# A column unit between FoX's turned probabilities and its values, and FoX's second tile and MoBA's turns at other places among the recurrence's column units

## The chip, the cores and the metric

The kernel runs on one core of one Trainium2 chip. The metric is the device time of one execution in microseconds. Before the change it is 1789.96 us, the median of three runs (1787.77 to 1790.02).

## The reference, cut to what matters

Two different transformer blocks, each with two layers, over a sequence of 256 tokens of width 1024, all in fp32. The edits lie in the mixer stage of the first block, which runs once in each of its two layers. There one projection of the normed input, `z = rms_norm(x, mix_norm[l]) @ mix_w_in[l]`, feeds three mixers side by side:

```python
z_fox, z_moba, z_rwkv = jnp.split(z, [FOX_IN, FOX_IN + MOBA_IN], axis=-1)
y_fox  = fox_mixer(z_fox, ...)    # 4 heads of 64: softmax(q k^T / 8 + c_i - c_j, causal) v
y_rwkv = rwkv7_mixer(z_rwkv, ...) # 8 heads of 64: a recurrence over tokens with decay and a rank-one correction
y_moba = moba_mixer(z_moba, ...)  # 4 heads of 64, rotary on 16 dims: at 256 tokens one causal block
y = jnp.concatenate([y_fox, y_rwkv, y_moba], axis=-1) @ mix_w_out[l]
```

For each of FoX and MoBA: scores of a tile of 128 queries, mask, softmax, product with the values. For the recurrence: r, k and v of width 512, each blended with the token before (`zf + (z_prev - zf) * mu`), then decays, normed keys, and the recurrence itself, which the kernel does in chunks of 64 tokens with small matmuls. Behind the mixers stand a projection with a residual, a cross attention and a feed-forward layer.

## The kernel before, in words

**Weights.** All large weights come as one stream of 546 units of up to 256 x 512 fp32 (512 KB). SP loads them into a ring of four places (`raw`). For each unit ScalarE copies it, rounded, to `whi` (`act_split`, L339) and VectorE writes the rest, `raw - whi`, to `wlo` (`dve_split`, L380). Each product is then three matmuls: high by high, high by low, low by high (L400 to L402; in a column unit L421 to L423). ScalarE's copy of unit u waits until TensorE has used unit u - 4; SP's load waits for VectorE's split of it.

**Tokens.** 256 tokens are two tiles of 128 (`t` or `qt` is 0 or 1).

**Column units.** The recurrence's k, r and v are projected turned, with channels on partitions: `pe_rw_cols(l, n, banks)` does unit n (0 to 3) of one of them, 24 matmuls of 128 x 256, into two PSUM banks. k and v use banks 0 and 1, r banks 4 and 5. After the four units of one, VectorE scales the two banks (`dve_rw_scale`, L993), ScalarE multiplies by 1 - mu (`act_rw_mix`, L1000) and VectorE adds the token before times mu (`dve_rw_mix`, L1009).

**FoX and MoBA.** A tile goes through these steps (`fox` True or False):

- TensorE turns queries and keys (`pe_at_turn`, L809, for FoX; `pe_mo_turn`, L1646, for MoBA, both into bank 6 for each tile, so the second waits until ScalarE has copied the first); ScalarE copies them out (L815).
- `pe_at_scores`: TensorE, L1707, and for FoX the forget term in L1711.
- `dve_at_scores`: VectorE scales and masks (L1725, and for the second tile L1728), row maximum (L822), its negative, the "shift" (L824).
- `act_at_exp`: ScalarE, four exponentials with row sums (L830).
- `pe_at_probs`: TensorE turns the probabilities (L844) in groups of four; ScalarE copies the even groups (`act_at_probs`, L851), VectorE the odd (`dve_at_probs`, L858, after the reciprocal of the sums, L863).
- `pe_at_values`: TensorE (L872), `dve_at_values`: VectorE multiplies by the reciprocals (L880).

**Keys of the recurrence.** `pe_rw_length` (L1083) sums squares, `dve_rw_keys_k` is one product of 128 x 1024 (L1117), `dve_rw_keys` makes the normed keys (L1126, four instructions, whose last MoBA's first turn waits for) and two products (L1132, L1136). After the column units come `pe_rw_products` (L1214) with masks on VectorE (L1227), then five levels of a triangular inverse (L1266, L1278, with L1285 on ScalarE and L1293 on VectorE), a bonus and gate part (L1424, L1436, L1437) and the chunks (L1312 and on).

**Order.** Every engine has its own list, written by hand, and runs it strictly in order: `pe_mix` (L2130), `act_mix` (L2238), `dve_mix` (L2340), `pool_mix`. The engines meet only by semaphores. No planner moves anything; an operation that waits holds all that stands behind it in its engine's list.

Of the kernel before, what the change touches and what calls it, by code (L numbers as in the profile page):

```python
# [131 lines left out]
class Program:  # L132
# [1997 lines left out]
    def pe_mix(self, l):  # L2130
        pe = self.nc.tensor
        for n in range(4):
            self.pe_rw_low(l, n)
            if n < 2:
                self.pe_turn_x(("mix", l), self.TURN_BANKS["mix"], self.x_done(l, "ffn1", 1), 4 + 2 * n, 2)
        self.pe_mix_spread(l)
        queries, keys, values = (self.pe_z(l, g) for g in (1, 2, 3))
        next(queries)
        self.pe_rw_low_turn(l)
        next(queries)  # L2140
        next(queries)
        self.pe_rw_lora(l)
        next(queries)
        self.pe_rw_cum(l, 0)
        self.pe_rw_cum(l, 1)
        for n in range(4):
            next(keys)
        for n in range(4):
            next(values)
        for sem, value in self.z_done(l, 2):  # L2150
            pe.wait_ge(sem, value)
        self.pe_rw_cols(l, 0, (0, 1))
        self.pe_rw_cols(l, 1, (0, 1))
        self.pe_at_turn(l, 0)
        self.pe_rw_cols(l, 2, (0, 1))
        self.pe_at_logs(l)
        self.pe_at_turn(l, 1)
        self.pe_rw_cols(l, 3, (0, 1))
        self.pe_at_scores(l, True, 0)
        pe.wait_ge(*self.rw_act("exp -cum", l, 0))  # L2160
        self.pe_rw_cols(l, 0, (4, 5))
        self.pe_rw_cols(l, 1, (4, 5))
        self.pe_rw_length(l)
        self.pe_at_probs(l, True, 0)
        self.pe_at_values(l, True, 0)
        self.pe_at_scores(l, True, 1)
        self.pe_rw_cols(l, 2, (4, 5))
        self.pe_rw_cols(l, 3, (4, 5))
        self.pe_mo_turn(l, 0)
        self.pe_at_probs(l, True, 1)  # L2170
        pe.wait_ge(*self.rw_dve("square sum", l, 1))
        self.pe_rw_cols(l, 0, (0, 1))
        self.pe_at_values(l, True, 1)
        self.pe_mo_turn(l, 1)
        self.pe_rw_cols(l, 1, (0, 1))
        self.pe_at_scores(l, False, 0)
        self.pe_rw_cols(l, 2, (0, 1))
        self.pe_rw_cols(l, 3, (0, 1))
        self.pe_at_probs(l, False, 0)
        self.pe_rw_products(l, 0, (0, 1))  # L2180
        self.pe_at_values(l, False, 0)
        self.pe_rw_products(l, 0, (2, 3))
        self.pe_at_scores(l, False, 1)
        self.pe_kv(l, 0, 0)
        self.pe_rw_products(l, 1, (0, 1, 2, 3))
        self.pe_kv(l, 0, 1)
        self.pe_at_probs(l, False, 1)
        self.pe_rw_by_token(l, "v", self.VT, (5, 7), [self.rw_dve("mixed", "v", l, 3), self.rw_dve("masked", l, 1, 1),
                                                      self.rw_dve("masked", l, 1, 3)])
        self.pe_at_values(l, False, 1)  # L2190
        self.pe_kv(l, 0, 2)
        self.pe_rw_level(l, 1)
        self.pe_rw_level(l, 2)
        self.pe_rw_by_token(l, "b", self.E3, (5, 7), [self.rw_act("by token", "v", l, 1), self.rw_dve("b end", l)])
        self.pe_rw_level(l, 3)
        self.pe_rw_by_token(l, "k", self.E2, (5, 7), [self.rw_act("by token", "b", l, 1), self.rw_dve("k end", l)])
        self.pe_rw_level(l, 4)
        self.pe_rw_bonus(l, 3)
        self.pe_rw_gate(l, 0, 2)
        self.pe_rw_level(l, 5)  # L2200
        pe.wait_ge(*self.rw_act("bonus", l))
        self.pe_rw_gate(l, 1, 3)
        self.pe_rw_first(l)
        self.pe_rw_early(l, 0, 0)
        self.pe_rw_u(l, 0, 0)
        self.pe_kv(l, 0, 3)
        self.pe_rw_state(l, 0, 0)
        self.pe_kv(l, 1, 0)
        self.pe_rw_rhs(l, 0, 1)
        self.pe_rw_early(l, 0, 1)  # L2210
        self.pe_rw_u(l, 0, 1)
        self.pe_kv(l, 1, 1)
        self.pe_rw_state(l, 0, 1)
        self.pe_kv(l, 1, 2)
        self.pe_rw_rhs(l, 1, 0)
        self.pe_rw_early(l, 1, 0)
        self.pe_rw_u(l, 1, 0)
        self.pe_kv(l, 1, 3)
        self.pe_rw_state(l, 1, 0)
        self.pe_kv_keys(l, 0)  # L2220
        self.pe_kv_keys(l, 1)
        self.pe_rw_rhs(l, 1, 1)
        self.pe_wo_a_turn(l, 0)
        self.pe_rw_u(l, 1, 1)
        self.pe_wo_a_turn(l, 2)
        self.pe_rw_state(l, 1, 1)
        self.pe_wo_a(l, 0, 0)
        self.pe_wo_a(l, 0, 1)
        self.pe_wo_a(l, 1, 0)
        self.pe_turn(("wo_b", l), [[self.Y[:, t, k * P:(k + 1) * P] for t in range(NT)] for k in range(4)], (4, 5, 6, 7),  # L2230
                     [self.rw_dve("out", l, 1)], kt0=4)
        self.pe_wo_a(l, 1, 1)
        self.pe_gemm((0, 1), 4, kt0=4, key=("wo_b", l), first=False)
        self.pe_gemm((2, 3), 4, kt0=4, key=("wo_b", l), first=False, units=(0,))
        self.pe_early("xa", l, self.x_done(l, "mix", 0))
        self.pe_gemm((2, 3), 4, kt0=4, key=("wo_b", l), first=False, units=(1,))

    def act_mix(self, l):  # L2238
# [45 lines left out]
        self.act_split(1)  # L2284
        self.act_mo_turn(l, 0)
        self.act_at_probs(l, True, 1)
        self.act_rw_mix(l, "r", self.RT, PV_OMR)
        self.act_split(2)
        self.act_mo_turn(l, 1)
        self.act_split(1)  # L2290
        self.act_at_exp(l, False, 0)
        self.act_split(1)
# [47 lines left out]
    def dve_mix(self, l):  # L2340
# [39 lines left out]
        self.dve_at_probs(l, True, 0)  # L2380
        self.dve_rw_length(l)
        self.dve_split(1)
        self.dve_at_values(l, True, 0)
        self.dve_rw_keys_k(l)
        self.dve_at_scores(l, True, 1)
        self.dve_rw_keys(l)
        self.dve_split(1)
# [1217 lines left out]
```

## Time and profile before

| | |
|---|---|
| median of three runs | 1789.96 us (1787.77 to 1790.02) |
| profiled execution | 1789.94 us, span 1788.6 us |
| TensorE, matmul | 1765.4 us busy, 99% of the span |
| TensorE, weight load | 1476.6 us, 83% |
| VectorE | 1155.0 us, 65% |
| ScalarE | 945.4 us, 53% |
| GpSimd | 128.3 us, 7% |
| mean granted TensorE clock | 0.998 |
| DMA | 301.12 MB, mean 168 GB/s |

Times are from the start of the span. Matmuls overlap in the pipe, so each one's duration is longer than its step to the next, and a busy TensorE is not one at its peak. The step from one start to the next is what counts in the timeline. In brackets behind an operation stands the idle time of its engine just before it and what ended it. The stretch with the edits is from about 262 to 300 us in layer 0 and lies 620 us later in layer 1.

### The profile page before, as it was taken

What the parts mean: (1) busy time and instruction counts of PE and PEld (TensorE: products, weight loads), DVE (VectorE), ACT (ScalarE), POOL (GpSimd) and SP (SyncE); (2) the same over time, 40 slices, a digit from 0 to 9 for tenths busy, and PEclk for the clock granted to TensorE, in tenths of its full rate; (3) what the DMA queues carried; (4) which work ended last, traced back from release to release, by engine and by line L of the source; (5) the groups of instructions that cost most, each with busy time, mean ns of one, the idle gap of its engine ahead of it and who ended that gap; (6) DMA issues with size and microseconds to landing.
All of it is one profiled execution on the core that took longest, in us unless ns stands there. A gap on an engine that the chain in (4) does not pass through costs nothing.

```text
span 1788.6 us, 26360 instructions
## 1 busy us (share of the span) xinstructions
PE 1765.4 (99%) x10762; PEld 1476.6 (83%) x10762; DVE 1155.0 (65%) x1589; ACT 945.4 (53%) x1433; POOL 128.3 (7%) x90
## 2 busy tenths in 40 slices
PE   9999999999999999999999999999999999999999
PEld 6888888888888888888888878888888888888887
DVE  5555678676555565556786755555697557697556
ACT  6454675345544454447653554444646554656553
POOL 0100010141000000000002210000002000002000
PEclk9999999999999999999999999999999999999999
DMA  8755542134555557555421436555554455554564
GB/s 285 279 190 186 173 152 85 61 105 130 187 185 186 186 187 253 186 169 188 142 84 61 140 116 223 189 188 170 165 180 156 166 193 193 174 177 153 174 190 130
DMA packets 84343, 301.12 MB, mean 168 GB/s; under 512 B 9728, under 2 KB 10880, under 8 KB 83712
## 3 DMA queue, kind: packets, MB, share of 16 engines
q1 hardware_dynamic: 80192, 289.44, 49.1%
q10 hardware_dynamic: 3712, 8.56, 1.4%
q8 instruction: 85, 1.39, 0.3%
q0 software_dynamic: 320, 1.45, 0.3%
q14 instruction: 34, 0.28, 0.0%
HBM read 298.36 MB, written 1.05 MB: 167 GB/s over the span
## 4 chain that ended last, share of the span: by engine, by line
PE 88%; DVE 6%; ACT 4%; issue 1%; DMA 1%; POOL 0%; SPq 0%; DVEq 0%; ACTq 0%
PE ps L400 25%; PE ps L402 25%; PE ps L401 25%; DVE wlo L380 1%; ACT whi L339 1%; PE ps L623 1%; PE ps L1278 1%; PE ps L1266 1%; DMA raw<-stream 1%; DVE a_lo L476 1%; PE ps L2680 1%; PE ps L809 1%; PE ps L460 1%; PE ps L423 1%; PE ps L421 1%
## 5 line engine op out<-in xcount | busy, mean ns | idle before, releaser
L380 DVE TENSOR_TENSOR wlo<-raw,whi 128x1024 fp32r<-128x1024 f32 (+1 forms) x545 | 668.9, 1236 | 360.1 <-ACT whi L339 358.6
L339 ACT ACTIVATE whi<-raw 128x1024 fp32r<-128x1024 f32 (+1 forms) x545 | 570.7, 1053 | 454.2 <-PE ps L402 423.7
L400 PE MATMUL ps<-whi,a_hi 128*128 128x512 f32 x1712 | 677.2, 396 | 5.9 <-DVE a_lo L2013 2.0
L402 PE MATMUL ps<-whi,a_lo 128*128 128x512 f32 x1712 | 664.7, 388 | 0.0
L401 PE MATMUL ps<-wlo,a_hi 128*128 128x512 f32 x1712 | 663.7, 388 | 0.0
L400 PEld LDWEIGHTS ps<-whi,a_hi 128*128 128x128 f32 x1712 | 321.5, 188 | 74.5 <-issue 4.7
L402 PEld LDWEIGHTS ps<-whi,a_lo 128*128 128x128 f32 x1712 | 321.3, 188 | 67.6
L401 PEld LDWEIGHTS ps<-wlo,a_hi 128*128 128x128 f32 x1712 | 321.9, 188 | 61.6
L400 PE MATMUL ps<-whi,h_hi 128*128 128x512 f32 x336 | 131.6, 392 | 0.0
L402 PE MATMUL ps<-whi,h_lo 128*128 128x512 f32 x336 | 130.9, 390 | 0.0
L401 PE MATMUL ps<-wlo,h_hi 128*128 128x512 f32 x336 | 130.8, 389 | 0.0
L400 PEld LDWEIGHTS ps<-whi,h_hi 128*128 128x128 f32 x336 | 63.1, 188 | 13.6 <-issue 0.7
L402 PEld LDWEIGHTS ps<-whi,h_lo 128*128 128x128 f32 x336 | 63.1, 188 | 13.2
L421 PE MATMUL ps<-a_hi,whi 128*128 128x256 f32 x256 | 73.9, 289 | 0.0
L401 PEld LDWEIGHTS ps<-wlo,h_hi 128*128 128x128 f32 x336 | 63.1, 188 | 12.9
L423 PE MATMUL ps<-a_hi,wlo 128*128 128x256 f32 x256 | 72.4, 283 | 0.0
L422 PE MATMUL ps<-a_lo,whi 128*128 128x256 f32 x256 | 72.3, 283 | 0.0
L645 ACT ACTIVATE arena<-ps,small 128x256 f32<-128x256 f32 x88 | 36.9, 471 | 65.6 <-PE ps L402 65.5
L553 POOL TENSOR_TENSOR small<-small,minus_half 128x2 f32<-128x2 f32 x9 | 6.3, 701 | 858.1 <-DVE small L546 642.3
L691 DVE SCALAR_TENSOR_TENSOR arena<-ps,small,arena 128x256 f32<-128x256 f32 x88 | 38.5, 480 | 38.4 <-ACT arena L645 38.4
L652 ACT ACTIVATE h_hi<-ps 128x256 fp32r<-128x256 f32 x72 | 23.7, 382 | 57.4 <-PE ps L623 57.4
L790 POOL TENSOR_TENSOR small<-small,minus_half 128x16 f32<-128x16 f32 (+1 forms) x14 | 39.2, 2803 | 166.3 <-DVE small L2622 80.5
(330 smaller groups left out, 1680.6 us busy)
## 6 DMA issues: line engine op xcount, KB each, us to landing
raw<-stream SPq DMA_DIRECT2D x545, 512.0 KB, 3.4
arena<-rows ACTq DMA_DIRECT2D x2, 1026.0 KB, 13.8
arena<-mem_turned ACTq DMA_DIRECT2D x2, 1024.0 KB, 9.1
arena<-lora ACTq DMA_DIRECT2D x2, 768.0 KB, 6.6
arena<-x_turned SPq DMA_DIRECT2D x4, 256.0 KB, 6.4
x_res<-x SPq DMA_DIRECT2D x2, 512.0 KB, 9.4
arena<-mem ACTq DMA_DIRECT2D x1, 1024.0 KB, 12.2
arena<-rows ACTq DMA_DIRECT2D x2, 512.0 KB, 4.6
```

The costliest lines, as they stand in the source:

```text
L339: self.split_hi.mark(act.activation(self.weights(self.whi, u), self.weights(self.raw, u), ACT.Copy), u)
L380: self.split_lo.mark(dve.tensor_tensor(self.weights(self.wlo, u), self.weights(self.raw, u), self.weights(self.whi, u).bitcast(F32), ALU.s ...
L400: pe.matmul(out, a_h, hi, start=start, stop=False, skip_group_check=True)
L401: pe.matmul(out, a_h, lo, start=False, stop=False, skip_group_check=True)
L402: last = pe.matmul(out, a_l, hi, start=False, stop=True, skip_group_check=True)
L421: pe.matmul(out, hi, self.AHI[:, kt, :], start=first and kt == 0, stop=False, skip_group_check=True)
L422: pe.matmul(out, hi, self.ALO[:, kt, :], start=False, stop=False, skip_group_check=True)
L423: last = pe.matmul(out, lo, self.AHI[:, kt, :], start=False, stop=True, skip_group_check=True)
L645: self.silu.mark(act.activation(self.SG[:, t, :], self.bank((2 if j == 1 else 4) + t, 256), ACT.Silu, scale=self.rs(0, t)), key, j, t)
L652: self.ht_hi.mark(act.activation(self.h_place(j)[0][:, kk, :], self.bank(self.h_bank(j, kk), S), ACT.Copy), key, j, kk)
L691: self.h_ready.mark(dve.scalar_tensor_tensor(self.h_buffer(j)[:, t, :], self.bank((2 if j == 1 else 4) + t)[:, 256:512], self.rs(0, t), se ...
L790: m.mark(pool.tensor_tensor(x, x, self.minus_half[:, 0:x.shape[1]], ALU.pow), key)
```

## The change

Only the order of calls in the three lists. On TensorE unit 2 of r is moved from behind FoX's second scores to between FoX's first turned probabilities and first values; unit 0 of v, with its wait, from behind FoX's second turned probabilities to before MoBA's first turn; and FoX's second values from before MoBA's second turn to behind unit 1 of v. On ScalarE the copy of MoBA's second turn goes from behind the blends of r and two splits to before them. On VectorE the product L1117 goes before FoX's first values.

```diff
@@ pe_mix
         self.pe_at_probs(l, True, 0)
+        self.pe_rw_cols(l, 2, (4, 5))
         self.pe_at_values(l, True, 0)
         self.pe_at_scores(l, True, 1)
-        self.pe_rw_cols(l, 2, (4, 5))
         self.pe_rw_cols(l, 3, (4, 5))
+        pe.wait_ge(*self.rw_dve("square sum", l, 1))
+        self.pe_rw_cols(l, 0, (0, 1))
         self.pe_mo_turn(l, 0)
         self.pe_at_probs(l, True, 1)
-        pe.wait_ge(*self.rw_dve("square sum", l, 1))
-        self.pe_rw_cols(l, 0, (0, 1))
-        self.pe_at_values(l, True, 1)
         self.pe_mo_turn(l, 1)
         self.pe_rw_cols(l, 1, (0, 1))
+        self.pe_at_values(l, True, 1)
         self.pe_at_scores(l, False, 0)
@@ act_mix
         self.act_at_probs(l, True, 1)
+        self.act_mo_turn(l, 1)
         self.act_rw_mix(l, "r", self.RT, PV_OMR)
         self.act_split(2)
-        self.act_mo_turn(l, 1)
@@ dve_mix
         self.dve_split(1)
+        self.dve_rw_keys_k(l)
         self.dve_at_values(l, True, 0)
-        self.dve_rw_keys_k(l)
         self.dve_at_scores(l, True, 1)
```

## Rows read from the trace of the kernel before

**Rows 1.** The page, busy us by engine (share of the span) x instructions.

```profile
PE 1765.4 (99%) x10762; PEld 1476.6 (83%) x10762; DVE 1155.0 (65%) x1589; ACT 945.4 (53%) x1433; POOL 128.3 (7%) x90
```

**Rows 2.** Chain of waits, 262 to 345 us: start us, us, what.

```profile
269.13 1.09 PE ps L1711 x8
...
270.31 0.42 DVE arena L1725
...
295.74 0.34 DVE arena L880
...
296.21 1.13 PE ps L1707 x8
```

**Rows 3.** Timeline of TensorE, layer 0: start us, us, operation [idle before, releaser].

```profile
265.61 0.60 PE L844 MATMUL ps<-const_tables,arena 128*128 128x128 f32 x4
266.99 1.08 PE L872 MATMUL ps<-arena 128*128 128x64 f32 x8 [0.78 <-ACT arena L851]
...
270.12 0.39 PE L421 MATMUL ps<-a_hi,whi 128*128 128x256 f32 x1
...
275.98 0.60 PE L1646 MATMUL ps<-const_tables,arena 128*128 128x128 f32 x4
276.41 1.04 PE L844 MATMUL ps<-const_tables,arena 128*128 128x128 f32 x8
...
280.15 1.89 PE L872 MATMUL ps<-arena 128*128 128x64 f32 x16
281.88 0.61 PE L1646 MATMUL ps<-const_tables,arena 128*128 128x128 f32 x4
...
285.70 0.71 PE L1707 MATMUL ps<-arena 64*128 64x128 f32 x8 [0.34 <-ACT arena L815]
...
292.21 0.60 PE L844 MATMUL ps<-const_tables,arena 128*128 128x128 f32 x4
...
296.21 1.13 PE L1707 MATMUL ps<-arena 64*128 64x256 f32 x8 [0.30 <-DVE arena L880]
```

**Rows 4.** Timeline of VectorE, layer 0.

```profile
270.31 0.42 DVE L1725 SCALAR_TENSOR_TENSOR arena<-ps,const_tables 128x256 f32<-128x256 f32 x1 [0.58 <-PE ps L1711]
...
273.10 1.67 DVE L1126 SCALAR_TENSOR_TENSOR arena<-arena 128x256 f32<-128x256 f32 x4
...
277.38 1.22 DVE L380 TENSOR_TENSOR wlo<-raw,whi 128x1024 fp32r<-128x1024 f32 x1
...
284.10 0.42 DVE L880 TENSOR_TENSOR arena<-ps,small 128x256 f32<-128x256 f32 x1
284.43 1.22 DVE L380 TENSOR_TENSOR wlo<-raw,whi 128x1024 fp32r<-128x1024 f32 x1
...
289.34 0.17 DVE L824 TENSOR_SCALAR small<-small 128x4 f32<-128x4 f32 x1
...
295.65 0.41 DVE L880 TENSOR_TENSOR arena<-ps,small 128x256 f32<-128x256 f32 x1
```

**Rows 5.** Timeline of ScalarE, layer 0.

```profile
276.61 0.60 ACT L815 ACTIVATE arena<-ps 128x512 f32<-128x512 f32 x1 [0.36 <-PE ps L1646]
```

**Rows 6.** Timeline of VectorE, layer 1.

```profile
890.45 0.42 DVE L1725 SCALAR_TENSOR_TENSOR arena<-ps,const_tables 128x256 f32<-128x256 f32 x1 [0.58 <-PE ps L1711]
```

**Rows 7.** Stretches: length, busy by engine, PEclk, DMA; then the chain of waits.

```profile
336.00:340.00 4.00, 4.00 (x82) 4.00 (x80) 0.26 (x1) 1.19 (x2) 0.00 (x0) 0.51 0.01 4
...
956.00:960.00 4.00, 4.00 (x72) 2.42 (x70) 2.56 (x3) 0.61 (x2) 0.00 (x0) 1.00 0.02 4
...
331.79 0.96 PE ps L1436 x2
...
342.89 1.01 PE ps L1312 x29
...
951.95 0.96 PE ps L1436 x2
...
959.95 1.01 PE ps L1312 x29
```

## The prediction

> **What bounds the kernel now.** I read the page's busy times first: TensorE's matmuls are busy for 1765.4 us, 99% of the span [rows 1]. That share says little about one stage, since a modelled end of a matmul covers short waits. So I read next the chain of waits through the mixers of layer 0, where all edits lie. It does not stay on TensorE. It leaves TensorE with the last matmul of FoX's scores for the second tile (L1711, ends 270.22), goes to VectorE (L1725, 270.31) and stays there, but for a few pieces of ScalarE that VectorE's own results released, until the normalised values of MoBA's first tile (L880, 295.74). There it returns to TensorE, with the scores of MoBA's second tile at 296.21 [rows 2]. So for 26 us the end is set by VectorE's queue, and its start by the moment at which TensorE delivers those FoX scores. The timelines say the same from both sides. VectorE sat idle for 0.58 us before L1725, on TensorE's L1711 [rows 4]. TensorE has three small holes: 0.78 us before FoX's first values (ScalarE's copy of the turned probabilities), 0.34 us before MoBA's first scores (ScalarE's L815, the copy of MoBA's turned tile 1), 0.30 us before MoBA's second scores (VectorE's L880) [rows 3]. Layer 1 has the same 0.58 us at 890.45 [rows 6]; one layer is worked out and doubled.
>
> **The change part by part.** No instruction, wait or DMA is added or dropped; the order on three queues changes. The weight units keep their order, so the split work and SP's queue of loads see the same sequence; POOL's queue is untouched.
>
> Edit 1, TensorE: column unit 2 of r goes between FoX's turned probabilities and values of tile 0. A unit takes 2.93 us: two of them fill 270.12 to 275.98 [rows 3]. Eight transposes and one unit take 276.41 to 280.15, 3.74 us, so a transpose takes 0.10 us [rows 3]. After the change the four transposes run from 265.61 to 266.0, the unit until 268.94. Its weights are ready: the unit's split stands ahead of the first FoX scores in VectorE's order. ScalarE's copy had ended by 266.99, where the values started before; they now start at 268.94 without a wait. The hole of 0.78 us is filled, which with the idle start of the pipe is 0.98 us of the unit's 2.93 us; the other 1.95 us stand in front. The values and the scores of tile 1 take the 3.13 us from 266.99 to 270.12 [rows 3]. So these scores end at 272.07 instead of 270.12.
>
> That is the step that costs. Before, the unit stood behind the scores and ran while VectorE scaled and reduced them. VectorE now starts L1725 at 270.31 + 1.95 = 272.26. Has it something to do meanwhile? Edit 2 moves its product k w (L1117) ahead of FoX's values; both ran before the scores anyhow, so nothing more is brought into the hole. I cost edit 2 at nothing: what hides it is the wait for the scores itself. Without that cover (had the values been late on the chain) it could cost or save up to its own 1.2 us; it is not late.
>
> Behind L1725 everything on VectorE is in order and moves with it: L1126 from 273.10 to 275.05, the split of the second v unit from 277.38 to 279.33, FoX's second values from 284.10 to 286.05, the split of the fourth v unit from 284.43 to 286.38, MoBA's shift from 289.34 to 291.29, MoBA's first values from 295.65 to 297.60 [rows 4]. The two waits for ScalarE that lie in between (blends of r, the split after MoBA's exponentials) follow pieces of this same chain and move too.
>
> Edit 3, TensorE, the rest: r's unit 3 runs 272.07 to 275.0, v's unit 0 to 277.93; then MoBA's turn 0, which needs L1126's four products (276.72 by the shift), 0.43 us to 278.36 [rows 3, 4]; FoX's eight transposes to 279.17. Turn 1 waits for ScalarE's copy of turn 0. Before, that copy began 0.63 us after the turn did and took 0.60 us [rows 3, 5]: 1.23 us against 0.43 + 0.81 = 1.24 us of turn and transposes, so the wait is between 0 and 0.2 us. Turn 1 ends near 279.6. Then v's unit 1 needs its split, which VectorE ends at 279.33 + 1.22 = 280.55: a new wait of 0.95 us. The unit ends at 283.5, the values of tile 1 (1.73 us, 280.15 to 281.88) at 285.2; VectorE wants them at 286.05, 0.8 us later. MoBA's first scores follow at once: turn 1 was copied long before, so the hole of 0.34 us goes. From 285.70 to 292.21 they and two units took 6.51 us [rows 3], now ending at 291.7; the fourth unit's split is ready at 287.6, a microsecond ahead of its use. Next come MoBA's transposes, which need exponentials that move by 1.95 us: TensorE waits, at most 1.95 + 0.5 = 2.4 us. MoBA's second scores then wait for L880 and start at 296.21 + 1.95 = 298.16.
>
> Edit 4, ScalarE: the copy of turn 1 goes ahead of the blends of r. Costed at nothing: ScalarE has nothing to do there until VectorE scales r, which is itself 1.95 us later. If TensorE were later than that, ScalarE would hold the blends, up to the 0.60 us of the copy.
>
> From 298.16 on TensorE runs without another of these waits, and all that VectorE and ScalarE bring it is shifted by the same amount, so nothing gives it back. Sum: 2 x 1.95 = 3.9 us. Bounds for a layer: nothing, if VectorE absorbs it; 2.93 us, if the filled hole brings nothing. I take 1.95 us, since both ends of the chain are read from rows. The profiled execution took 1789.94 us around its span and the median of the runs is 1789.96 us, so the base needs no correction: 1789.94 + 3.9 = **1793.8 us**.
>
> **The rivals.** *R1, TensorE's own stream decides.* If VectorE's queue had more air than its records show, only TensorE's holes count. The change fills 0.78 and 0.34 us, and with 0.30 us if VectorE is in time, 1.42 us a layer, 2.8 us in all: 1787.1 us. For it: TensorE's 99%. Against: the chain leaves TensorE exactly at the scores, and the 0.30 us show VectorE behind TensorE at the end of the stretch. It decides once the scores' delay stays under VectorE's slack; the row of 0.58 us shows that slack to be below zero.
>
> *R2, absorbed.* The later scores are made good inside the stretch, by about what the filled holes give, or the two effects cancel: 1790 us. For it: six queue places change at once and half a microsecond here and there is not in my sum. Against: no queue gets shorter.
>
> *R3, the clock.* In layer 0 the granted clock was 0.51 from 336 to 340 us, TensorE's lower level of 1.2 GHz, and 1.00, its 2.4 GHz, at the same place of layer 1 [rows 7]. The same work took 342.89 - 331.79 = 11.10 us in layer 0 and 959.95 - 951.95 = 8.00 us in layer 1 [rows 7]. Ahead of both stood the same run of 64x64 matmuls, so it is a matter of when this work comes, and the change moves it by 1.95 and 3.9 us. One fall is worth 3.1 us: none makes 1793.8 - 3.1 = 1790.7 us, two make 1796.9 us. For it: two layers alike in all but this; and the runs shown reach from 1787.77 to 1790.02, a step of 2.2 us. Against a lasting effect: it would be drawn anew in each run, and the median would keep to the commoner number. The Trainium skill (TensorE: Matmul & The Clock Gate, "What's actually happening") says that the gate follows how busy the array has been, and looks at it on a schedule that runs freely and does not start with the kernel. By that rule identical work may fall or not, as the trace's two layers do, and the time is 3.1 us lower or higher by the draw alone, as R3.
>
> **How the numbers follow.** This kernel's measurement can tell 0.2%, 3.6 us, from no change; my 3.9 us lie just above it. Chances: forecast with one fall as before 0.52; R3 with none 0.15, with two 0.10; R2 0.13; R1 0.10. Of the forecast's 0.52, 0.42 come out slower by more than 3.6 us and 0.10 within. Slower: 0.42 + 0.10 (two falls) = 0.52. Within: 0.10 + 0.15 + 0.13 + 0.03 (part of R1) = 0.41. Faster: 0.07, R1 with a fall less. The range leaves out R1 and what lies beyond two falls: 1789.5 to 1797.0 us. The forecast's own range is 1792.5 to 1795.5.
>
> **What would show it.** In the changed profile, in each layer: no wait before L872 at about 269, where the 0.78 us stood; L1711 ends 1.9 to 2.0 us later against L844 at 265.6, and the idle time of VectorE before L1725 is about 2 us, in two parts (before L880, and before L1725); a new wait of some 1 us before the first L421 behind the second turn, on VectorE's split; no wait on L815 before MoBA's scores; a wait of 1 us or more on ScalarE's L830 before MoBA's transposes; the one on L880 grows from 0.30 us to about 1 us; the first L1266 comes 1.95 us later in layer 0 and 3.9 us later in layer 1. I am wrong if the first L1266 comes at its old place or earlier (R1, R2), or if it comes as said and the end doesn't (R3).

## The result and the profile after

The changed kernel takes 1791.74 us, the median of 19 runs (1789.75 to 1793.65), against 1787.77 us for the kernel before (1786.22 to 1791.12, 19 runs). The ratio is 1.0019 with a 95% interval of 1.0013 to 1.0025: slower by 3.4 us, 2.3 to 4.5. The change is clear of no change, but lies at the prediction's line of 0.2%, 3.6 us, and not clearly on either side of it. The profiled execution took 1791.55 us, with a span of 1790.2 us.

The best measure here is a stretch within one profile, from the first L1083 (sums of squares) to the first L1266 (the triangular inverse). All edits lie in it, and the granted clock was 1.00 throughout it in both kernels.

| start, us | first L1083 | first L1266 | stretch |
|---|---|---|---|
| before, layer 0 | 263.88 | 311.41 | 47.53 |
| before, layer 1 | 884.02 | 931.57 | 47.55 |
| changed, layer 0 | 263.46 | 312.82 | 49.36 |
| changed, layer 1 | 882.33 | 931.69 | 49.36 |

The four rows of layer 0, TensorE's timeline, the kernel before first:

```profile
263.88 1.89 PE L1083 MATMUL ps<-arena,const_tables 128*128 128x256 f32 x8
311.41 2.08 PE L1266 MATMUL ps<-arena 64*64 64x64 f32 x64
...
263.46 1.89 PE L1083 MATMUL ps<-arena,const_tables 128*128 128x256 f32 x8
312.82 2.08 PE L1266 MATMUL ps<-arena 64*64 64x64 f32 x64
```

So the change costs 1.83 us in layer 0 and 1.81 us in layer 1, 3.6 us in all. None of it is given back behind the stretch: from the first L1083 of layer 0 to that of layer 1 the changed kernel takes 882.33 - 263.46 = 618.87 us, and turn_early, one of the experiments below, 880.65 - 263.68 = 616.97 us. Its stretch is within 0.03 us as long as that of the kernel before, and its granted clock was 1.00 from one L1083 to the other, as that of the changed kernel was.

The timeline of TensorE in the changed kernel, layer 0; the columns are start, length, operation, and in brackets the idle time before it and what ended it.

```profile
265.19 0.60 PE L844 MATMUL ps<-const_tables,arena 128*128 128x128 f32 x4
265.55 0.36 PE L421 MATMUL ps<-a_hi,whi 128*128 128x256 f32 x1
...
268.50 1.00 PE L872 MATMUL ps<-arena 128*128 128x64 f32 x8
...
271.56 0.39 PE L421 MATMUL ps<-a_hi,whi 128*128 128x256 f32 x1
...
277.41 0.60 PE L1646 MATMUL ps<-const_tables,arena 128*128 128x128 f32 x4
277.84 1.04 PE L844 MATMUL ps<-const_tables,arena 128*128 128x128 f32 x8
278.71 0.64 PE L1646 MATMUL ps<-const_tables,arena 128*128 128x128 f32 x4
...
280.08 0.39 PE L421 MATMUL ps<-a_hi,whi 128*128 128x256 f32 x1 [0.73 <-DVE wlo L380]
...
283.05 1.89 PE L872 MATMUL ps<-arena 128*128 128x64 f32 x16
284.87 0.72 PE L1707 MATMUL ps<-arena 64*128 64x128 f32 x8
...
292.67 0.66 PE L844 MATMUL ps<-const_tables,arena 128*128 128x128 f32 x4 [1.14 <-ACT arena L830]
...
297.63 1.13 PE L1707 MATMUL ps<-arena 64*128 64x256 f32 x8 [1.20 <-DVE arena L880]
```

The two holes of [rows 3] that the change aimed at are gone: no wait before L872, none on L815 before MoBA's scores. Three waits stand there now: 0.73 us for the split of v's unit 1, 1.14 us for the exponentials, and 1.20 us instead of 0.30 for MoBA's first values. From the turned probabilities to the end of FoX's second scores it is 271.56 - 265.19 = 6.37 us instead of 270.12 - 265.61 = 4.51 us [rows 3], 1.86 us more. The same stretch on VectorE:

```profile
267.73 1.22 DVE L1117 TENSOR_TENSOR arena<-arena 128x1024 f32<-128x1024 f32 x1
269.61 0.42 DVE L880 TENSOR_TENSOR arena<-ps,small 128x256 f32<-128x256 f32 x1 [0.67 <-PE ps L872]
271.75 0.42 DVE L1725 SCALAR_TENSOR_TENSOR arena<-ps,const_tables 128x256 f32<-128x256 f32 x1 [1.71 <-PE ps L1711]
...
274.53 1.67 DVE L1126 SCALAR_TENSOR_TENSOR arena<-arena 128x256 f32<-128x256 f32 x4
...
285.52 0.42 DVE L880 TENSOR_TENSOR arena<-ps,small 128x256 f32<-128x256 f32 x1
...
297.07 0.41 DVE L880 TENSOR_TENSOR arena<-ps,small 128x256 f32<-128x256 f32 x1
```

VectorE idles 0.67 + 1.71 us where it idled 0.58 us [rows 4]: 1.80 us more, which is the loss but for a few hundredths. Behind it the queue is as before, shifted: from L1725 to MoBA's first L880 it is 297.07 - 271.75 = 25.32 us, before 295.65 - 270.31 = 25.34 us [rows 4]. The chain of waits (start, us, what) hands over at the same operations as in [rows 2]:

```profile
270.57 1.09 PE ps L1711 x8
...
271.75 0.42 DVE arena L1725
...
297.15 0.34 DVE arena L880
...
297.63 1.13 PE ps L1707 x8
...
312.89 2.01 PE ps L1266 x64
```

### The profile page after: what moved, and what is told of

Same layout as the page of the kernel before. It is cut to its first block, busy times and chain, and to the rows that moved or that the text cites. A ratio compares the mean times of both kernels' runs of the same rounds, so it can differ in the third digit from the quotient of the medians.

```text
span 1790.2 us, 26360 instructions
## 1 busy us (share of the span) xinstructions
PE 1764.3 (99%) x10762; PEld 1475.6 (82%) x10762; DVE 1156.0 (65%) x1589; ACT 945.2 (53%) x1433; POOL 128.2 (7%) x90
## 4 chain that ended last, share of the span: by engine, by line
PE 89%; DVE 6%; ACT 3%; issue 1%; DMA 1%; POOL 0%; SPq 0%; DVEq 0%; ACTq 0%
PE ps L400 25%; PE ps L402 25%; PE ps L401 25%; DVE wlo L380 1%; PE ps L623 1%; PE ps L1278 1%; DMA raw<-stream 1%; PE ps L1266 1%; PE ps L421 1%; ACT whi L339 1%; PE ps L422 1%; PE ps L423 1%; DVE a_lo L476 1%; PE ps L2680 1%; PE ps L809 1%
## 5 line engine op out<-in xcount | busy, mean ns | idle before, releaser
L421 PEld LDWEIGHTS ps<-a_hi,whi 128*128 128x128 f32 x256 | 48.9, 191 | 3.2 <-DVE wlo L380 1.9
```

What stands on the lines that cost most here:

```text
L421: pe.matmul(out, hi, self.AHI[:, kt, :], start=first and kt == 0, stop=False, skip_group_check=True)
```

## The experiments

Each changes the order of calls in the lists, and nothing else. The stretch is given for layers 0 and 1. Ratios are to the kernel before on the same chip, with their 95% intervals.

| kernel | stretch, us | ratio (interval) |
|---|---|---|
| kernel before | 47.53, 47.55 | |
| whole change | 49.36, 49.36 | 1.0019 (1.0013 to 1.0025) |
| unit_only | 49.40, 49.39 | 1.0019 (1.0010 to 1.0028) |
| unit_back | 49.36, 49.35 | 1.0024 (1.0015 to 1.0032) |
| two_units | 53.11, 52.51 | 1.0053 (1.0040 to 1.0066) |
| product_early | 47.53, 47.52 | 1.0002 (0.9993 to 1.0010) |
| v0_only | 49.36, 49.34 | 1.0017 (1.0008 to 1.0026) |
| values_late | 48.94, 48.95 | 1.0011 (1.0002 to 1.0020) |
| turn_early | 47.50, 47.55 | 1.0001 (0.9992 to 1.0010) |
| key_product_late | 48.10, 48.06 | 1.0004 (0.9995 to 1.0013) |
| scores_first_both | 47.52, 47.56 | 1.0006 (0.9997 to 1.0015) |
| scores_first_turn | 48.29, 46.97 | 1.0003 (0.9994 to 1.0012) |

**unit_only: edit 1 alone.**

```diff
         self.pe_at_probs(l, True, 0)
+        self.pe_rw_cols(l, 2, (4, 5))
         self.pe_at_values(l, True, 0)
         self.pe_at_scores(l, True, 1)
-        self.pe_rw_cols(l, 2, (4, 5))
```

> The kernel before with edit 1 alone: r's unit 2 between FoX's first turned probabilities and first values. Theory: the stretch from the first L1083 to the first L1266 is 49.3 to 49.4 us in both layers, as with the whole change, time 3.6 us over before where the clock is alike (ratio about 1.002). Rival A (the later moves carry the cost): 47.5 us, ratio 1.000. Rival B (the unit costs more and the later moves give some back): over 49.7 us, ratio 1.0025 or more.

As the theory had it: 49.40 and 49.39 us. Without edit 2 VectorE waits 1.80 us before L880 and 0.58 us before L1725, the same sum as in the whole change, so edit 2 is worth nothing. VectorE's timeline:

```profile
269.90 0.42 DVE L880 TENSOR_TENSOR arena<-ps,small 128x256 f32<-128x256 f32 x1 [1.80 <-PE ps L872]
272.04 0.42 DVE L1725 SCALAR_TENSOR_TENSOR arena<-ps,const_tables 128x256 f32<-128x256 f32 x1 [0.58 <-PE ps L1711]
```

**unit_back: the whole change without edit 1.**

```diff
         self.pe_at_probs(l, True, 0)
-        self.pe_rw_cols(l, 2, (4, 5))
         self.pe_at_values(l, True, 0)
         self.pe_at_scores(l, True, 1)
+        self.pe_rw_cols(l, 2, (4, 5))
         self.pe_rw_cols(l, 3, (4, 5))
```

> The changed kernel with r's unit 2 back behind FoX's second scores; every other move stays. Measure: the stretch from the first L1083 to the first L1266, 47.53 us before and 49.36 us changed in layer 0. Theory (the unit ahead of the scores delays VectorE's chain, the other moves cost nothing): 47.4 to 47.6 us, VectorE idle 0.6 us before L1725, the wait of 0.78 us before L872 back, and a time like that of the kernel before (ratio 0.999 to 1.001). Rival A (the later moves, with their new waits on the split of v's unit 1, the exponentials and L880, carry the cost): still 49.0 us or more, ratio 1.001 to 1.002. Rival B (the later moves gain what the unit takes away from them): 46.9 to 47.2 us, ratio 0.999 or less.

The theory's first half fails here: the stretch stays at 49.36 us, as rival A had it, though unit_only shows edit 1 to cost the whole sum too. The number is rival A's, but the wait is not one of the three that it named. VectorE's timeline shows a wait at a place where before there was none:

```profile
269.71 0.42 DVE L1725 SCALAR_TENSOR_TENSOR arena<-ps,const_tables 128x256 f32<-128x256 f32 x1 [0.61 <-PE ps L1711]
...
279.76 0.69 DVE L858 COPY arena<-ps 128x512 f32<-128x512 f32 x1 [1.69 <-PE ps L844]
```

The scores come in time, but now three column units stand on TensorE between them and FoX's turned probabilities, and L858, next in VectorE's queue, waits 1.69 us for these.

**v0_only and values_late: which of the later moves it is.** They split edit 3. The first moves v's unit 0 alone, the second the rest, with edit 4.

```diff
 v0_only, pe_mix
+        pe.wait_ge(*self.rw_dve("square sum", l, 1))
+        self.pe_rw_cols(l, 0, (0, 1))
         self.pe_mo_turn(l, 0)
         self.pe_at_probs(l, True, 1)
-        pe.wait_ge(*self.rw_dve("square sum", l, 1))
-        self.pe_rw_cols(l, 0, (0, 1))
 values_late, pe_mix (and act_mo_turn(l, 1) ahead of act_rw_mix)
         self.pe_at_probs(l, True, 1)
+        self.pe_mo_turn(l, 1)
...
-        self.pe_at_values(l, True, 1)
-        self.pe_mo_turn(l, 1)
         self.pe_rw_cols(l, 1, (0, 1))
+        self.pe_at_values(l, True, 1)
```

> The kernel before with one move alone: v's unit 0 (with its wait) ahead of MoBA's turn 0 and FoX's second turned probabilities; r's unit 2 and everything else stay. The theory as corrected by the undo run: whatever stands on TensorE ahead of an operation that VectorE's queue is waiting for costs its length less VectorE's air at that place. Here VectorE wants the turned probabilities for L858 at 278.6, and TensorE would bring them at about 280.2: the stretch from the first L1083 to the first L1266 is 49.1 to 49.4 us, with some 1.6 us idle before L858 and the other waits as before; ratio 1.0015 to 1.0025. Rival (the cost in the undo run came from FoX's second values behind v's unit 1, or from the turn): 47.5 us, ratio 1.000.

> The kernel before with the rest of the later moves: MoBA's turn 1 right behind FoX's second turned probabilities, its copy on ScalarE ahead of the blends, and FoX's second values behind v's unit 1; v's unit 0 stays behind the turned probabilities. Theory: TensorE ends the values at about 285.3 by the clock of the kernel before, VectorE wants them for L880 at 284.1, so VectorE waits 1.2 to 1.3 us before that L880 and the stretch is 48.7 to 48.9 us; ratio 1.001 to 1.002. Rival (the values' place is free, as VectorE has other work): 47.2 to 47.5 us, ratio 0.9995 to 1.000.

Both as expected (values_late by 0.04 us above the expected 48.7 to 48.9 us), each with one new wait of VectorE and no other. In v0_only:

```profile
279.98 0.69 DVE L858 COPY arena<-ps 128x512 f32<-128x512 f32 x1 [1.68 <-PE ps L844]
```

In values_late:

```profile
285.67 0.42 DVE L880 TENSOR_TENSOR arena<-ps,small 128x256 f32<-128x256 f32 x1 [1.33 <-PE ps L872]
```

So three moves cost 1.86, 1.8 and 1.4 us a layer when each stands alone (edit 1, unit 0 of v, the late values), and all together they cost 1.83. They don't add: each delays another meeting point of the same two queues, and a queue that is already late is not made later by what comes in time for the late hour. unit_back shows it without edit 1: unit 0 of v and the late values together cost 1.83 us, not 3.2.

**turn_early: what is left of edits 3 and 4.** As values_late, but the values ahead of v's unit 1, where they were.

> The kernel before with one move alone: MoBA's turn 1 right behind FoX's second turned probabilities, its copy ahead of the blends of r; FoX's second values stay where they were. Theory (VectorE's chain gates, this touches only TensorE's wait of 0.34 us): the wait on L815 goes, the stretch stays at 47.5 us, and TensorE's wait before MoBA's second scores or transposes takes it up; ratio 0.9995 to 1.0005. Rival (this move has a part of the cost, by TensorE's wait for the copy of turn 0 or ScalarE's order): 47.8 us or more.

As expected: 47.50 and 47.55 us. The 0.34 us on L815 is gone and TensorE's wait on L880 grew by nearly as much, from 0.30 to 0.62 us:

```profile
296.00 1.13 PE L1707 MATMUL ps<-arena 64*128 64x256 f32 x8 [0.62 <-DVE arena L880]
```

**two_units: a double dose.** The kernel before with units 2 and 3 of r between the turned probabilities and the values.

```diff
         self.pe_at_probs(l, True, 0)
+        self.pe_rw_cols(l, 2, (4, 5))
+        self.pe_rw_cols(l, 3, (4, 5))
         self.pe_at_values(l, True, 0)
         self.pe_at_scores(l, True, 1)
-        self.pe_rw_cols(l, 2, (4, 5))
-        self.pe_rw_cols(l, 3, (4, 5))
```

> The kernel before with units 2 and 3 of r both between FoX's first turned probabilities and first values, a double dose. Theory: the second unit finds no hole to fill, so it costs its full 2.9 us: FoX's second scores come 4.8 us later than before, the stretch is 52.2 to 52.4 us, and the time is 9.5 us over before (ratio about 1.0053). Rival (VectorE has air that swallows part, or TensorE's stream decides): the second unit costs less than 2 us a layer, stretch under 51.4 us.

The second unit costs its whole length: VectorE's L1725 starts 11.17 us behind the first L1083 in both layers, in unit_only 8.29 us, so 2.88 us later. But both stretches are longer than the expected 52.2 to 52.4 us, since more is lost behind L1725: 52.51 us in layer 1 is 3.12 us over unit_only, and 53.11 us in layer 0 is 3.71 us over it. With both units gone ahead, TensorE has nothing to run while VectorE works on the scores, in either layer, and then starts at a lower clock. TensorE's timeline, two rows of layer 0 and one of layer 1:

```profile
278.98 1.08 PE L1646 MATMUL ps<-const_tables,arena 128*128 128x128 f32 x4 [4.72 <-DVE arena L1126]
279.85 1.92 PE L844 MATMUL ps<-const_tables,arena 128*128 128x128 f32 x8
...
901.59 1.09 PE L1646 MATMUL ps<-const_tables,arena 128*128 128x128 f32 x4 [4.72 <-DVE arena L1126]
```

Stretch, length, busy time of TensorE, its weight loads, VectorE, ScalarE and GpSimd, the granted clock, DMA:

```profile
280.00:288.00 8.00, 8.00 (x54) 8.00 (x52) 6.88 (x11) 3.77 (x8) 0.00 (x0) 0.70 0.45 131
```

After 4.72 us idle the same four transposes take 1.08 us instead of 0.60, the eight 1.92 instead of 1.04 [rows 3], and the mean clock of 280 to 288 us is 0.70. Layer 1 fell too, but for less long: over the 8 us from the start of L1646 the mean clock is 0.72 there and 0.64 in layer 0. The layer with the longer fall lost the more. In layer 0 VectorE then waits 0.23 us for a unit of v and 0.28 us for L1214 (before L993 at 297.70 and L1227 at 299.21), and in unit_only for neither. That the whole surplus is the clock's is read from the traces and not shown: none of the five runs of this order kept a mean clock of 1.000.

**product_early: is it VectorE's load?**

```diff
 dve_mix
         self.dve_at_scores(l, True, 0)
         self.dve_split(1)
+        self.dve_rw_keys_k(l)
         self.dve_at_probs(l, True, 0)
...
-        self.dve_rw_keys_k(l)
         self.dve_at_scores(l, True, 1)
```

> The kernel before with VectorE's product L1117 moved from ahead of FoX's second scores to the idle microsecond before L863 (after the split behind FoX's first scores). Theory (the scores' arrival from TensorE gates the chain): nothing changes, stretch 47.4 to 47.6 us, and the idle time before L1725 grows from 0.58 us to about 1.7 us; ratio 0.999 to 1.001. Rival (the amount of work in VectorE's queue gates it): the stretch shrinks by up to 1.1 us a layer, ratio 0.9988 to 0.9995.

As the theory had it: nothing moves, and VectorE's idle time before L1725 grows from 0.58 us to

```profile
269.94 0.43 DVE L1725 SCALAR_TENSOR_TENSOR arena<-ps,const_tables 128x256 f32<-128x256 f32 x1 [1.71 <-PE ps L1711]
```

Up to L1725, then, the arrival of TensorE's scores gates VectorE, not its own load.

**key_product_late: the load further on.**

```diff
 dve_mix
-        self.dve_rw_keys_end(l)
         self.dve_at_probs(l, False, 0)
...
         self.dve_rw_products(l, 0, (2, 3))
+        self.dve_rw_keys_end(l)
```

> The kernel before with one product of 1.2 us (L1142, which nothing needs soon) moved in VectorE's queue from ahead of MoBA's first values to behind the masks that follow them. Theory: VectorE's chain to L880 is 1.1 us shorter, but TensorE is only 0.30 us behind it, so 0.30 us a layer is gained and TensorE's stream takes over: stretch 47.2 to 47.3 us, no wait before MoBA's second scores, the 0.34 us on L815 stays; ratio 0.9995 to 1.000. Rival A (VectorE's load sets the end beyond this point too): 46.4 us. Rival B (it is paid back behind): 47.5 us.

Wrong, by all three: 48.10 and 48.06 us, slower by 0.5 us. VectorE's timeline says why the first half failed:

```profile
291.15 0.18 DVE L863 RECIPROCAL small<-small 128x4 f32<-128x4 f32 x1 [0.59 <-ACT arena L830]
292.09 1.23 DVE L380 TENSOR_TENSOR wlo<-raw,whi 128x1024 fp32r<-128x1024 f32 x1 [0.77 <-ACT whi L339]
```

L1142 had stood in VectorE's wait for ScalarE's exponentials and the split behind them. Taken away, it left 1.04 us more idle time and moved nothing: MoBA's second scores came 32.31 us after the first L1083, before 32.33 us. Where it was put, it delayed all that follows on VectorE, among it the low part of the memory's last rows (L1794), which now ended at 308.87; TensorE's third memory unit waits for it and began at 308.93, which by the first L1083 is 0.5 us later than in the kernel before.

**scores_first_both and scores_first_turn: a version that would beat both.** If the scores of FoX's second tile are what VectorE waits for, they should go ahead of FoX's first values.

```diff
 pe_mix
         self.pe_at_probs(l, True, 0)
-        self.pe_at_values(l, True, 0)
         self.pe_at_scores(l, True, 1)
+        self.pe_at_values(l, True, 0)
 dve_at_scores, ahead of dve_max; the call in dve_mix goes
+        if fox and qt:
+            self.dve_at_values(l, True, 0)
```

Both hold this, product_early and turn_early; scores_first_both holds key_product_late as well.

> Meant as a version better than both: in the kernel before, FoX's second scores ahead of FoX's first values on TensorE, with VectorE's L880 for those values between its masking and its row maximum; L1117 in VectorE's idle microsecond before L863; L1142 late as in the run above; MoBA's turn 1 and its copy early, the second values where they were. Theory: VectorE's chain is 0.7 + 1.1 us shorter and falls behind TensorE's, which loses its waits of 0.34 and 0.30 us: stretch 46.8 to 47.0 us, 0.6 to 0.7 us a layer gained, TensorE's 0.78 us before the scores stays; ratio 0.9990 to 0.9998. Rival (another wait takes their place): 47.3 us or more.

> The better version without the late L1142: in the kernel before, FoX's second scores ahead of FoX's first values on TensorE, L880 for those values between VectorE's masking and its row maximum, L1117 in the idle microsecond before L863, MoBA's turn 1 and its copy early. L1142 stays where it was, since the last runs showed that it fills VectorE's wait for the exponentials and that it delays the split before the third memory unit when it comes late. Theory: MoBA's second scores come 0.55 us earlier, as in the last version, and nothing is paid back: stretch 46.9 to 47.1 us, about 1.1 us gained in both layers; ratio 0.9990 to 1.0002. Rival (L1142 had hidden a gain of VectorE's there, or another wait pays back): 47.3 us or more.

The first gains 0.55 us up to MoBA's second scores (31.78 us after the first L1083 instead of 32.33) and pays it back behind, as key_product_late does: 47.52 and 47.56 us, as the rival had it. The second shows in layer 1 what was expected, 46.97 us, but in layer 0 it took 48.29 us, since the granted clock fell in the stretch. The first row is scores_first_turn:

```profile
268.00:274.00 6.00, 6.00 (x40) 5.64 (x37) 4.80 (x11) 4.74 (x11) 0.00 (x0) 0.72 0.26 87
```

The kernel before had 1.00 there. By the time nothing is gained: ratio 1.0003 (0.9994 to 1.0012). None of its 11 runs kept a mean clock of 1.000, while 9 of the 21 runs of the kernel before on the same chip did. In scores_first_both, whose order on TensorE is the same, 1 of 11 did, while 12 of 33 of the kernel before did on that chip. Together that is 1 of 22 against 21 of 54, rarer than a draw from the same odds would readily give. So the new order may bring falls of the clock, but no run shows how. Where they lie only one profile of each shows: that of scores_first_both has none in the stretch. No version beat the kernel before.

## Why the prediction was right and where it was wrong

**Right: where the end is set, and by what.** The forecast said that VectorE's queue from L1725 on sets the end and that edit 1 delays its start by 1.95 us. Measured: 1.86 us by the first L1083 (271.75 - 263.46 against 270.31 - 263.88), 1.83 us in the stretch. The sum of 3.9 us stands against 3.6 us by the profiles and 3.4 us (2.3 to 4.5) by the ratio. The difference of 0.09 us in that delay lies in the prediction's terms: the values and scores were taken at the 3.13 us they took behind a wait, and without one took 271.56 - 268.50 = 3.06 us; the four transposes took 0.36 us and not 0.40; the unit took 2.95 us and not 2.93. The bound of 2.93 us a layer for a hole that brings nothing wasn't needed: the hole did take up 0.98 us of the unit.

**Right: the new waits.** The wait on the split of v's unit 1 was forecast at 0.95 us and is 0.73 us: the row counts it from the modelled end of MoBA's turn 1 (279.35), and VectorE's shift was 1.86 and not 1.95 us; the one on the exponentials was to be at most 2.4 us and is 1.14; the one on L880 about 1 us and is 1.20. The late values stayed hidden: VectorE came to them with no wait.

**Right only under cover: edits 3 and 4 at nothing.** The sum took these at nothing and called their cost hidden, without a price for the case that the cover is gone. The expectation of unit_back then made "costs nothing" out of "is hidden". The runs put prices in its place: v's unit 0 ahead of the turned probabilities 1.8 us a layer, the late values 1.4 us, the early turn and its copy nothing. They are covered by edit 1's own delay. The time came out right, since the whole change has that delay, but the sentence on cover, which the prediction gave for edits 2 and 4, was missing for the one that needed it.

**Wrong: one of the signs.** The first L1266 was to come 1.95 us later in layer 0 and 3.9 us later in layer 1, and its old place was to mean that the forecast is wrong. It came 1.41 us later (312.82 against 311.41) and 0.12 us later (931.69 against 931.57), in layer 1 all but at its old place. The sign compared places in two executions, as if nothing else differed between them. The changed kernel's first L1083 came 0.42 us earlier (in the twelve profiles it lies anywhere from 263.21 to 264.05 us), and the kernel before had lost 3.10 us to the clock in layer 0: 3.64 - 0.42 - 3.10 = 0.12 us. The stretch within one profile has neither in it.

**Wrong: the base, and the size of a fall.** The forecast of 1793.8 us lies 2.1 us above the 1791.74 us measured, which is also below the forecast's own range of 1792.5 to 1795.5 us; only the whole range, made wide for R3, holds it. The size of the change is not the reason (3.9 against 3.6 us): the base was the median of three runs, 1789.96 us, and over 19 runs it is 1787.77 us. The likely cause is R3's fall of the clock, which the prediction priced at 3.1 us and took as present "as before". In the later comparisons, 9 of 21, 12 of 33 and 17 of 29 runs of the kernel before kept a mean clock of 1.000; their median is 1786.5 us. The seven runs of the changed kernel with a mean clock of 1.000 have a median of 1790.26 us, so without falls the difference is 3.7 us.

Nor is 3.1 us the size of every fall. From the first L1436 to L1312 the twelve profiles (of both kernels and the ten experiments), two layers each, show three lengths: 8.0 us in 13 cases, 9.5 to 9.6 us in 9, 11.1 us in 2. So a fall there cost 1.5 or 3.1 us, and R3's "none" and "two" were not the only other draws. In the changed kernel's profile the fall lies in layer 1 instead of layer 0 (0.76 from 952 to 956 us), layer 0 is free of it, and it cost 961.61 - 952.06 - 8.00 = 1.55 us:

```profile
332.00:336.00 4.00, 4.00 (x43) 2.48 (x44) 1.24 (x2) 0.78 (x2) 0.00 (x0) 1.00 0.24 92
952.00:956.00 4.00, 4.00 (x43) 2.48 (x44) 0.14 (x1) 0.78 (x2) 0.00 (x0) 0.76 0.01 2
...
952.06 0.96 PE ps L1436 x2
...
961.61 1.01 PE ps L1312 x29
```

So the spans of the two profiles, 1788.6 and 1790.2 us, differ by only 1.6 us, and the stretches by 3.6: whoever compares spans alone would halve the effect. By the Trainium skill (TensorE: Matmul & The Clock Gate, "What's actually happening") the gate looks at the array on a schedule of its own that doesn't start with the kernel, so such a draw is to be expected. The traces agree in that the fall behind L1436 came in layer 0 alone in 2 of the twelve profiles, in layer 1 alone in 3, in both in 3 and in neither in 4. That it is blind to the order of work they don't show, and the 1 of 22 runs above speak against it.

**The rivals.** R1 (TensorE's stream decides) is refuted by turn_early, where one of its holes goes and the stretch stays. R2 (absorbed) is refuted by unit_only and two_units, where the dose comes out whole.

## What to carry to other kernels

Before filling a hole of the busiest engine, see whose queue the chain of waits enters behind it: here 0.78 us of TensorE's idle time (0.98 us with the start of the idle pipe) were filled with a unit of 2.93 us, and the 1.9 us left over stood in front of the one result that VectorE was waiting for. Long independent work belongs directly behind the operation that feeds the other queue, not before it, and only as much of it as ends before that queue wants its next result: a third unit in that place cost 1.8 us. Costs of moves along one chain don't add: each has to be priced with the others taken out, or an undo run will look like a refutation. And where single executions differ by a clock that falls at random, compare a stretch between two fixed operations.

## What the runs showed of the hardware that was not expected

The fall of the clock is not bound to the stretch of 64x64 matmuls where [rows 7] shows it: in scores_first_turn it came also at 268 to 274 us (0.72), amid values and a full unit, behind a hole of 0.78 us that the kernel before has too, at a clock of 1.00. In two_units it followed a wait of 4.72 us in both layers. In that stretch of 64x64 matmuls the same work took one of three lengths, 8.0, 9.5 to 9.6 or 11.1 us, though in the kernel before TensorE's longest wait from 311 us to the fall at 332 to 340 us was 0.21 us.
